# Loads of w_ada into the homes of q, k and v, and another order of small steps, in the head of a one-core transformer block

## What is computed

```python
sc = jax.nn.silu(c)
mod = (sc @ w_ada + b_ada)[:, None, :]
sh1, sc1, ga1, sh2, sc2, ga2 = jnp.split(mod, 6, axis=-1)
h = rmsnorm(x, g_pre_mix) * (1.0 + sc1) + sh1
proj = h @ w_in
uv = jax.nn.gelu(proj[..., :2 * D_GMLP]); u, v = uv[..., :D_GMLP], uv[..., D_GMLP:]
q, k, vv = jnp.split(proj[..., 2 * D_GMLP:], 3, axis=-1)
o_sb = stick_breaking_attention(to_heads(q), to_heads(k), to_heads(vv))
o_g = gmlp_spatial_gating(u, v, ln_sgu_g, ln_sgu_b, w_spatial, b_spatial)
mixed = jnp.concatenate([rmsnorm(o_g, g_branch[:D_GMLP]), rmsnorm(o_sb, g_branch[D_GMLP:])], axis=-1)
x = x + ga1 * rmsnorm(mixed @ w_out, g_post_mix)
h = rmsnorm(x, g_pre_ffn) * (1.0 + sc2) + sh2
y = moe_ffn(h, ...)       # sigmoid router, top 8 of 64 experts in groups, a shared expert
x = x + ga2 * rmsnorm(y, g_post_ffn)
```

## Time and profile before

| | us |
|---|---|
| median of 3 runs | 1158.3 (1158.2 to 1160.55) |
| the profiled execution, its own time | 1162.7 |
| its span in the trace | 1161.0 |
| PE busy in the span | 1059.8 (91%) |
| DVE, ACT, POOL busy | 752.2, 575.4, 502.0 |
| PE busy from 405 to 1080 us (the experts' loop) | 674.5 of 675.0 |
| PE idle in front of a product that waited for a low part, 48 to 165 us | 14.6 in 3 waits |
| PE idle in front of `values_mm` for a pair's low part | 20.3 in 3 waits |
| mean granted TensorE clock, of full speed | 0.959 |

### The profile page before, as it was taken

The page is one execution under the profiler, slowest core; times in us unless marked ns, Lnnn a source line. Parts: engine busy times, 40 slices in busy tenths (PEclk is TensorE's granted clock), DMA queues, the critical chain, the costliest instruction groups (busy, mean ns, idle before and its releaser), DMA issues.

```text
span 1161.0 us, 14525 instructions
## 1 busy us (share of the span) xinstructions
PE 1059.8 (91%) x4508; PEld 725.5 (62%) x4508; DVE 752.2 (65%) x1276; ACT 575.4 (50%) x602; POOL 502.0 (43%) x210
## 2 busy tenths in 40 slices
PE   4898699678886899999999999999999999999966
PEld 0686567345654476677666677666677666677622
DVE  1555674543387577777777777777777777777338
ACT  5331154643224355666655566655566655566311
POOL 1231110330023166655566655566655566655400
PEclk9798889889899999999999999999999999999989
DMA  9576821101116279999999999999999988998387
GB/s 344 207 273 242 294 99 72 74 1 59 59 55 235 88 265 359 355 354 362 377 376 363 376 352 360 349 363 368 368 365 335 350 329 337 351 365 332 114 336 314
DMA packets 66695, 318.66 MB, mean 274 GB/s; under 512 B 16944, under 2 KB 17456, under 8 KB 39152
## 3 DMA queue, kind: packets, MB, share of 16 engines
q1 hardware_dynamic: 41936, 269.50, 60.2%
q0 software_dynamic: 22624, 45.40, 10.7%
q10 hardware_dynamic: 2112, 3.45, 0.9%
HBM read 317.25 MB, written 39.85 MB: 308 GB/s over the span
## 4 chain that ended last, share of the span: by engine, by line
PE 76%; DVE 10%; DMA 9%; issue 2%; ACT 2%; SPq 1%; DVEq 0%; POOLq 0%; POOL 0%; ACTq 0%
PE ps L1319 20%; PE ps L1300 11%; PE ps L1302 10%; PE ps L1301 10%; PE ps L983 7%; DMA ada<-in_w_ada_dram 4%; DMA yall<-y_rows 3%; PE ps L1053 3%; PE ps L1072 2%; PE ps L1163 2%; PE ps L1106 2%; DVE acc L1449 2%; PE ps L999 1%; PE ps L1136 1%; PE ps L1233 1%
## 5 line engine op out<-in xcount | busy, mean ns | idle before, releaser
L597 POOL DMA_INDIRECT hg<-h_rows,idxg x70 | 352.4, 5035 | 145.6 <-DVE idxg L1772 143.2
L1778 DVE TENSOR_TENSOR wlo<-raw,whi 128x2048 fp32r<-128x2048 f32 x134 | 300.5, 2283 | 0.0
L875 ACT ACTIVATE whi<-raw 128x2048 fp32r<-128x2048 f32 x136 | 261.4, 1923 | 2.3 <-DMA raw<-in_w_up_dram 2.3
L1319 PE MATMUL ps<-rawd,actt 128*128 128x512 f32 x544 | 244.5, 592 | 1.4 <-ACT actt L900 1.4
L1300 PE MATMUL ps<-whi,hthi 128*128 128x512 f32 x544 | 225.9, 415 | 0.0
L1302 PE MATMUL ps<-whi,htlo 128*128 128x512 f32 x544 | 213.8, 393 | 0.0
L1301 PE MATMUL ps<-wlo,hthi 128*128 128x512 f32 x544 | 213.3, 392 | 0.0
L1792 DVE TENSOR_TENSOR htlo<-ps,hthi 128x1024 fp32r<-128x1024 f32 x68 | 83.3, 1225 | 177.0 <-ACT hthi L896 177.0
L906 ACT ACTIVATE ysb<-ps 128x1024 f32<-128x1024 f32 x68 | 69.6, 1024 | 213.5 <-PE ps L1319 213.5
L1319 PEld LDWEIGHTS ps<-rawd,actt 128*128 128x128 f32 x544 | 102.8, 189 | 104.7 <-issue 97.8
L605 POOL DMA_INDIRECT y_rows<-ysb,idxs x68 | 73.2, 1077 | 161.0 <-ACT ysb L906 156.1
(11 more groups left out here) (262 smaller groups left out, 1290.8 us busy)
## 6 DMA issues: line engine op xcount, KB each, us to landing
raw<-in_w_gate_dram SPq DMA_DIRECT2D x68, 1024.0 KB, 8.3
raw<-in_w_up_dram SPq DMA_DIRECT2D x68, 1024.0 KB
rawd<-in_w_down_dram SPq DMA_DIRECT2D x68, 1024.0 KB
ada<-in_w_ada_dram SPq DMA_DIRECT2D x24, 1024.0 KB, 8.6
yall<-y_rows SPq DMA_DIRECT2D x8, 2048.0 KB, 22.8
wraw<-in_w_in_dram POOLq DMA_DIRECT2D x8, 1024.0 KB, 8.6
woraw<-in_w_out_dram SPq DMA_DIRECT2D x4, 1024.0 KB, 8.0
xs<-in_x_dram SPq DMA_DIRECT2D x4, 512.0 KB, 5.6
```

What stands on the lines that cost most here:

```text
L597: gp.indirect_dma_start(out=hg[s][:, :, :].rearrange("p k q -> p (k q)"), out_offset=None, in_=h_rows, in_offset=bass.IndirectOffsetOnAxis ...
L875: A(whi[:, s, :, cols], raw[:, s, :, cols], ACT.Copy).then_inc(hi_ok, 1)
L1319: ins = mm(bank(4 + hf), actt[:, k, :], rawd[:, s, k, hf * 512:(hf + 1) * 512], start=(k == 0), stop=(k == KF - 1))
L1778: V.tensor_tensor(wlo[s][:, :, c0:c1], raw[:, s, :, c0:c1], whi[:, s, :, c0:c1].bitcast(F32), ALU.subtract).then_inc(lo_dve, 1)
```

## The change

- **Loads of w_ada.** `ADA_SLOT` spreads pieces 8 to 23 over six slots: slots 3, 4, 5 (112, 120 and 128 KB: the later homes of `qt`, `kt` and `vv`) and 2 (136 KB, `v_sb`) are used again, and 1. A load waits for whoever used its slot last (`ada_last`), the first load of slots 6 and 7 for the transposes of `z1`. `evacuate(g)` and `sigmoids(0)` wait until the pieces that lie in their homes are weighed.
- **DVE's order.** One `piece_low` for each two pieces, each ahead of them where it can be; `mod_row` stands two pieces earlier for ga1. `grow` two and three are loaded by ACT.
- **PE's order.** `modulation_row(3)` stands behind `project(5)`; `modulation_row(5)` goes to banks 3 and 4 (`MOD_BANK`), between `u_chunk(0)` and `u_chunk(1)`, which no longer wait for ga2; `weights_tr(0)` does.
- **Pairs.** `pair_out` stands ahead of the `sigmoids` of the next odd head and `pair_low` ahead of its `attend`.
- **Fillers.** `FILL`: the `out_g` come two in slots 4 and 5, one in slots 6, 7 and 8, and the last behind slot 8.
- **Router.** It uses bank 0 in place of 2, and `shared_up(1)` moves from ahead of it to behind it.

The count of instructions that compute is the same.

```diff
-        ADA_SLOT = [0, 1, 2, 3, 4, 5, 0, 1] + [6 + n % 2 for n in range(FIRST, 24)]
+        ADA_SLOT = [0, 1, 2, 3, 4, 5, 0, 1, 2, 3, 4, 5, 1, 6, 7, 2, 1, 6, 7, 2, 1, 6, 7, 1]
+        def ada_last(n):
+            return max(i for i in range(n) if ADA_SLOT[i] == ADA_SLOT[n])
+        MOD_BANK = {2: 6, 3: 6, 4: 6, 5: 3}
+        FILL = {4: ((0,), (1,)), 5: ((2,), (3,)), 6: ((), (4,)), 7: ((), (5,)), 8: ((6,), ())}
...
-                if n in (6, 7):
-                    sp.wait_ge(sh_mm, n - 5)
-                elif n == FIRST:
+                if ADA_SLOT[n] >= 6 and n < 15:
                     sp.wait_ge(h1_tr, KD)
-                elif n >= FIRST + 2:
-                    sp.wait_ge(ada_used, n - 5)
...
+                elif n >= 6:
+                    m = ada_last(n)
+                    if m < FIRST // 2:
+                        sp.wait_ge(sh_mm, m + 1)
+                    else:
+                        sp.wait_ge(ada_used, m - 3)
...
             def evacuate(g):
+                ac.wait_ge(ada_used, (6, 7, 8, 16)[g])
...
             def sigmoids(h):
                 ac.wait_ge(z_mm, h + 1)
+                if h == 0:
+                    ac.wait_ge(ada_used, 19)
...
+            pair_out(0)
             sigmoids(3)
...
             for h in range(4, HEADS):
-                n = 2 * (h - 4)
+                if h % 2 == 1:
+                    pair_out((h - 3) // 2)
                 sigmoids(h)
-                og_out(n)
+                for n in FILL[h][0]:
+                    og_out(n)
                 weights_out(h - 1)
-                og_out(n + 1)
+                for n in FILL[h][1]:
+                    og_out(n)
                 if h < 6:
                     wo_high(h - 2)
-                if h % 2 == 1:
-                    pair_out((h - 3) // 2)
             weights_out(HEADS - 1)
+            og_out(6)
             pair_out(3)
+            og_out(7)
...
             project(4)
+            project(5)
             modulation_row(3)
-            project(5)
             project(6)
             modulation_row(4)
             project(7)
-            modulation_row(5)
...
             for h in range(HEADS + 1):
                 if h < HEADS:
                     scores_mm(h)
-                filler(h, 0)
+                    filler(h, 0)
+                if h == 0:
+                    modulation_row(5)
+                elif h == 1:
+                    pe.wait_ge(row_ok, 4)
                 if h >= 1:
                     weights_tr(h - 1)
+                if h == HEADS:
+                    filler(h, 0)
                 filler(h, 1)
                 if h >= 1:
                     values_mm(h - 1)
+            out_g(2 * TT - 1)
...
             h2_transposes(1)
-            shared_up(1)
             pe.wait_ge(wr_in, 16)
...
             router(3)
+            shared_up(1)
             shared_tr(0)
...
             piece_low(1)
+            weigh(8, 9)
             piece_low(2)
-            weigh(8, 9, 10)
+            weigh(10, 11)
...
             piece_low(3)
-            weigh(11, 12, 13)
+            weigh(12, 13)
+            v.wait_ge(row_in, 16 * 7)
+            mod_row(2, ga1, 1, False)
             piece_low(4)
             weigh(14, 15)
-            v.wait_ge(row_in, 16 * 7)
-            mod_row(2, ga1, 1, False)
             piece_low(5)
             weigh(16, 17)
             mod_row(3, a2, 2, True)
+            piece_low(6)
             weigh(18, 19)
-            piece_low(6)
+            piece_low(7)
             weigh(20, 21)
-            piece_low(7)
-            weigh(22, 23)
             mod_row(4, b2, 0, False)
             piece_low(8)
+            weigh(22, 23)
+            piece_low(9)
             mod_row(5, ga2, 3, False)
-            piece_low(9)
...
+            pair_low(0)
             gated_low(0)
             gated_low(1)
             attend(3)
...
-            pair_low(0)
             for h in range(4, HEADS):
-                attend(h)
                 if h % 2 == 1:
                     pair_low((h - 3) // 2)
+                attend(h)
```

More of the change, by code:

```diff
@@ L798, in _ @@
             piece_high(5)
+            ac.wait_ge(row_ok, 1)
+            ac.dma_start(grow[:, :], g_pre_ffn.partition_broadcast(P)).then_inc(grow_in, 16)
             piece_high(6)
@@ L801, in _ @@
             piece_high(7)
+            ac.wait_ge(row_ok, 2)
+            ac.dma_start(grow[:, :], g_post_ffn.partition_broadcast(P)).then_inc(grow_in, 16)
             piece_high(8)
@@ L931, in _ @@
             ac.wait_ge(lg_mm, 1)
-            A(scores[:, :, :], ps[:, 2 * BANK:2 * BANK + TT * E].rearrange("p (t e) -> p t e", t=TT),
+            A(scores[:, :, :], ps[:, 0:TT * E].rearrange("p (t e) -> p t e", t=TT),
               ACT.Sigmoid).then_inc(sig_ok, 1)
@@ L1027, in modulation_row @@
                 pe.wait_ge(acc_ok, ch)
-                if ch > 2:
+                if 2 < ch < 5:
                     pe.wait_ge(row_ok, ch - 2)
                 for hf in range(2):
-                    ins = mm(bank(6 + hf), ones[:, :], acc[:, ch % 2, hf * 512:(hf + 1) * 512],
+                    ins = mm(bank(MOD_BANK[ch] + hf), ones[:, :], acc[:, ch % 2, hf * 512:(hf + 1) * 512],
                              start=True, stop=True)
@@ L1057, in u_chunk @@
             def u_chunk(n):
-                if n < 2:
-                    pe.wait_ge(row_ok, 4)
-                else:
+                if n == 0:
+                    pe.wait_ge(row_ok, 3)
+                elif n >= 2:
                     pe.wait_ge(u_ev, n - 1)
@@ L1099, in out_g @@
                 if n < 2:
-                    pe.wait_ge(og_lo, 3 + n)
+                    pe.wait_ge(og_lo, 4)
                     pe.wait_ge(wolo_ok, 2)
@@ L1177, in filler @@
                     gated_tr(2 * part + 1)
-                elif h < HEADS:
-                    out_g(2 * (h - 4) + part)
+                else:
+                    for n in FILL[h][part]:
+                        out_g(n)
             for h in range(HEADS + 1):
@@ L1499, in mod_row @@
                 if plus_one:
-                    ins = V.scalar_tensor_tensor(out=dst[:, :], in0=bank(6, 2), scalar=1.0, in1=dst[:, :],
+                    ins = V.scalar_tensor_tensor(out=dst[:, :], in0=bank(MOD_BANK[ch], 2), scalar=1.0, in1=dst[:, :],
                                                  op0=ALU.add, op1=ALU.add)
                 else:
-                    ins = V.tensor_tensor(dst[:, :], bank(6, 2), dst[:, :], ALU.add)
+                    ins = V.tensor_tensor(dst[:, :], bank(MOD_BANK[ch], 2), dst[:, :], ALU.add)
                 if gain:
```

9 lines of the change are left out of this document (1 added, 8 removed).

## The result

| | before | changed |
|---|---|---|
| median, us | 1159.25 | **1141.09** |
| lowest and highest, runs | 1158.2 to 1160.55, 4 | 1140.54 to 1143.4, 4 |
| profiled execution, us | 1162.7 | 1143.4 |
| its span, us | 1161.0 | 1141.7 |
| mean granted clock | 0.959 | 0.963 |

The ratio of the times is 0.9847, with an interval of 0.9828 to 0.9866: the change gains 18.2 us, where 27.2 were forecast, and the time lies 0.1 us above the range of 1122 to 1141. The direction is right; 9 us of the gain are missing.

What follows compares the result with a forecast made beforehand. PE bounds the kernel; the loop from 405 us stays unchanged, so gains lie ahead of it: 34.0 us, less 4 for half clocks and 2.8 in the router, is 27.2, from 1158.3 to 1131 us, range 1122 to 1141.

Steps and rivals of the forecast that it cites:

- the three waits with their half clocks: Attention, ahead of values_mm: PE's waits of 8.23, 8.58 and 3.45 us go, with 1.5, 1.6 and 2.2 of half clock.
- Rival D: Slots 3 or 5: pairs' low parts still late, one gain of about 10 us stays out; 1141 us, chance 0.09.
- Rival C: Loads of w_ada land late and bind again, DVE holds a low part in each pair; 1162 us, chance 0.04.
- the new waits: PE idle ahead of project(4), project(6), u_chunk(2) (2.8 us, for u_out(0)) and weights_tr in slots 6 and 7 (2.45).
- the router's term: Router: shared_up(1) ahead of shared_tr(0) makes the sigmoid 7.0 us later, tables' chain waits 2.7; 2.8 lost with POOL's stalls.
- half clocks in new places: Idle times in slots 1, 6 and 7: between nothing and 8 us lost to PE's half clock; middle taken, 4.
- the maxima: Router, DVE beside POOL's subtractions: by the skill's rule they slip through uncontended, and the loss would be near 2.2 us.
- the ledger: Cumulative gains along PE's order through projection and attention: 34.0 us at out_s(0), 30.0 after 4 for half clocks.
- Rival A: Cold slots: half clock in full at all new idle places; gain 20 us, 1138 us, chance 0.20.
- the tail: Behind the last values_mm: two out_g fill waits of 1.33 and 2.78 us, out_s(0) begins warm, 2.4 us.
- rival O: From the experiments: missing time was lost earlier, in the loads' new slots or the rest of the order; no chance given.

Runs made afterwards that it cites:

- pairs_alone: Kernel before with only the pairs' high and low parts first in their slot, first two out_g waiting for all four gated low parts: 1138.04 us, ratio 0.9826.
- pairs_back: Changed kernel with the pairs' high parts on ACT and low parts on DVE at their old places, behind the slot's other work: 1167.45 us, ratio 1.0066.
- the two single runs: shared_up(1) put back ahead of router(0) in the changed kernel: 1133.5 us; only the router's part of the change in the kernel before: 1168.52 us.
- router_back: Changed kernel with shared_up(1) in its old place, ahead of router(0): 1133.5 us, ratio 0.978.
- warm_router: Changed kernel with unread products in PE's two idle times of the router's part, three behind router(0), six behind router(1): 1135.19 us, ratio 0.9792.
- up_twice: Changed kernel with the eight products of shared_up(1) done once more, unread, in the old place: 1142.25 us, ratio 0.9852.
- fill_back: Changed kernel with the eight out_g again two to a slot in slots 4 to 7, none behind the last values_mm: 1139.6 us, ratio 0.9836.
- all_three: Changed kernel with shared_up(1) back ahead of router(0), piece_low(4) and (6) ahead of rows ga1 and a2, row ga2 behind attend(0): 1121.5 us, ratio 0.9673.
- two_slots: Changed kernel with pieces 8 to 23 of w_ada in two slots in turn, as before: 1143.85 us, ratio 0.9872.

## Why the prediction was right and wrong

**Right: what bounds the kernel, and the largest term.** The pair's late low parts were the main thing: 22 to 26 us by `pairs_alone` and `pairs_back`. The forecast had 9.7 + 10.1 + 5.65 for the three waits with their half clocks, less 2.4 in slot 4: 23. From slot 2 to the first `og` it is 25.3 in the traces (111.2 us in the kernel before, 85.9 in `pairs_alone`). Rival D did not come: no `values_mm` waits. That its 1141 is the time measured is luck. Rival C did not come either.

**Right: the new waits.** Row and low part ahead of `project(4)` (3.81 idle), `project(6)` (3.79), `u_out(0)` (2.72, forecast 2.8), `out_g(0)` (0.91) and slots 6 and 7 (2.50, forecast 2.45).

**Wrong: the router's term**, 2.8 us lost, from a sigmoid that is ready 7.0 us later and had 4.4 to spare. Measured 9.0 from the first `og` to the loop (27.7 to 18.7), 7.6 and 8.9 by the two single runs. The step that failed is the place that `shared_up(1)` left, in the sentence **"Its old place cost nothing, since the last tile's x on DVE was later"**. It is true of PE's waiting: `h2_transposes(3)` starts 14.5 us behind the last `og`, before 14.8. It is not true of the clock. Out of its old place, `shared_up(1)` left 5.43 + 3.64 us of idle PE with only transposes and narrow products between, and the forecast, which has a paragraph on half clocks in new places, put nothing for this one and gave no reason. In the landmarks the 9.0 are:

- 3.8 until the router's end (gain 27.7 to 23.9): `h2_transposes(3)` 1.97 instead of 1.09, 32 router products 6.72 instead of 3.53. A part of this comes in the old place too: `router_back` took 6.17 for the 32.
- 3.6 from there to `posb` (23.9 to 20.3), which is what the 2.8 was for. Half of it is the clock again: `shared_up(1)` took 8.66 instead of 6.9, so DVE waited 4.55 us and not 2.7. With the clock back, in `warm_router` and `pairs_back`, the wait is 2.81 and the loss 1.8. The stalls beside POOL sum to 8.0, before to 8.7.
- 1.6 from there to the loop: `shared_up(3)` took 8.67 instead of 6.97, behind an idle time of 2.15 us. In `pairs_back` it took 6.97 behind 2.17.

So of some 9 us about 7 are the clock and 1.8 the order, for which 2.8 were forecast, or 2.2 if the maxima slip through, as they did: the wait was sized right, and the term for the clock was missing.

**Right: the maxima beside POOL.** By the Trainium skill, "SBUF — State Buffer", section "Who interferes with whom", a DVE instruction with at most one input in SBUF, outside the two-port modes, doesn't contend with GpSimd. The trace agrees: POOL subtracts from 346.44 on, and the four maxima begun at 346.17 took 0.61 us together, as they did alone in the kernel before, while `sel` behind them, with two inputs, took 3.54. A MATCH_REPLACE8 at 347.47 took 0.21, as alone. But most of the stalls was not saved: two instructions further on took them, 8.0 us against 8.7.

**A little off: the half clocks in new places.** The middle of 0 and 8 was taken, 4. At `out_s` 25.4 us are gained, where the ledger (34.0 without the 2.4 of `out_s(0)`, less 4) has 27.6; so 2.2 more, about 6 in all, if all of the gap is the clock. Half clocks stand at `u_chunk(0)` (6.90 instead of 5.45), `u_chunk(2)` (7.36), `project(6)` (13.78, had 12.77) and the `out_g` behind the idle time at 247.15. The waits were right and slot 2 still started only 3.1 us earlier than before instead of 7.7; the next slots took it back in part. But this is one of the slower executions. With the same order in the head, slot 2 starts at 193.0 in `up_twice` and 193.7 in `warm_router`, which is 5.8 and 5.2 us earlier than before, and `u_chunk(0)` takes 5.67 and 5.64. The lower bound, nothing, was badly founded too: behind the wait of 2.78 us in the earlier trace rows the granted clock of the kernel before was 0.51 from 302 to 307 us, the very half clock that the forecast counts as 2.4 at `out_s(0)`. Rival A, with all half clocks in full and 3.5 for the router, has 1138, the nearest of the rivals that came at least in part; its 2 us for a row's gains that land late did not show, since the two DVE instructions of each row stand 0.02 us apart in the chain.

**Wrong in its reason: the tail.** `out_s(0)` was to begin warm (2.4 us) because the two `out_g` fill the waits of 1.33 and 2.78 us. It did begin warm, but it does so in `fill_back` as well, with both waits open. The spreading was to gain 0.3 us in each of slots 6 and 7 and lose 0.3 behind them; in the traces slot 6 takes 13.1 us with it and 11.65 without (an `out_g` of 4.18 us behind the idle 2.50), slot 7 as long as without, and slot 8 to `out_s(0)` 10.15 and 8.8, so that it costs 2.8 in all in this pair of traces. The medians (1141.09 and 1139.6, intervals that meet) can't tell this from nothing.

**A slip in the sum.** 25.1 + 2 x 0.3 + 3.45 + 2.2 is 31.35, not 31.8; the forecast is high by less than half a microsecond for it.

2.3 at the first `og` (30.0 forecast, 27.7 there), which is all that rival O gets, and 9.0 - 2.8 = 6.2 in the router's part are 8.5, and the landmark of the loop misses the forecast by as much (27.2 - 18.7). What stays open is what decides the clock behind such waits. With the same two waits of 2.4 us the last router products ran at 2.4 GHz in the traces of before and `pairs_alone`, and mostly or all at 1.2 GHz in those of `router_back` and `all_three`. Behind the same 3.79 us `project(6)` took 13.78 us in the changed kernel, 12.49 in `up_twice` and 11.16 in `two_slots`. Each kernel has one trace, and single executions differ.

## What to carry to other kernels

Before an instruction is moved away from in front of a wait, ask what the engine does there instead: here dense products that merely filled a wait cost nothing, and taking them out cost twice, once in the clock of what follows the wait and once where they now stand. When a step makes PE's clock the question, look at every idle time that the change leaves, not only at those it adds in the part under study, and test it with products that nothing reads: if they pay, it was the clock. See in the trace that they fill the wait and don't overrun it, here by 2.3 us. And look for the steps that a change gives away: here one step of it, alone, gained as much (22.1 us) as the whole (18.2), by intervals that meet, and three small moves of its own instructions gained as much again (19.6).

## What the runs showed of the hardware

- Nine products that nobody reads, put into idle times, gave 5.9 us back by the medians, 3.6 of them in the router's part of the trace; in `up_twice` eight gave none, and an idle time of 2.44 us behind them stayed open, with the clock at 0.60 behind it.
- The clock after short waits isn't settled by the wait's length: behind two waits of 2.4 us it stayed at 1.00 in the kernel before and in `pairs_alone` and was 0.50 in `all_three` and 0.61 in `router_back`. Behind 5.4 and 3.6 us, in one and the same order, 32 router products took 6.72 us in the changed kernel and 4.38 in `pairs_back`.
- Beside POOL's subtraction of 128x2048, a two-input instruction of 128x256 took 3.54 us (0.42 alone, in the kernel before) and a cast to bf16 4.48 (0.29 alone), in one and the same trace in which four MAX8 took 0.61 together.
